# Fewer barriers between the spans of a two-layer decoder, and the next span's norm computed inside the down projection

## Chip, cores and metric

The kernel runs on one Trainium2 chip, on 8 cores at once. Each core works on two of the 16 batch entries and shares nothing with the others but the memory that they read from. The metric is the device time in microseconds (us) of the slowest core. Engines are named as in the profile: PE is TensorE's matmuls, PEld its weight loads, DVE VectorE, ACT ScalarE, POOL GpSimd, SP SyncE.

## What is computed

Two decoder layers over 2064 positions (16 meta tokens and 2048 inputs), width 1024. The reference, cut down:

```python
def hybrid_layer(h, ...):
    hn = rmsnorm(h, g_mix)
    z = hn @ w_in
    u, c_q, c_kv, k_rope, gate_a, gate_b = jnp.split(z, IN_OFFSETS, axis=-1)
    a = pool_mixer(u, pool_w, pool_scale)          # causal means over 2, 4, 8, 16 positions, then 128x128 products
    ...                                            # q, k, v from the normed latents, rope
    b = mla_attention(q_nope, q_rope, k_nope, k_rope, v)
    merged = jax.nn.sigmoid(gate_a) * (a @ w_pa) + jax.nn.sigmoid(gate_b) * (b @ w_pb)
    h = h + merged @ w_o
    hn = rmsnorm(h, g_ffn)
    h = h + (jax.nn.silu(hn @ w_gate) * (hn @ w_up)) @ w_down
    return h
# after both layers: rmsnorm(h, final_norm_g)[:, N_META:]
```

`rmsnorm` divides by the root of the mean square over the 1024 channels and multiplies by a gain.

## The kernel before

`hT` holds the state of one batch entry transposed, channels on the partitions (8 chunks of 128) and positions on the free axis, in float32, and stays on the chip. For each of the two entries and each of the two layers there are three phases:

1. Latents (lines 404 to 451): the norm and the latent projections, in blocks of 512 positions.
2. Attention (lines 455 to 547), head by head.
3. Pooling mixer, merge and feed-forward (lines 551 to 687), in three spans of 688 positions, each of two blocks of 344. A span does: the mixer norm (`norm_span(SM_GMIX)`, line 571); the pooling input projection (64 matmuls, lines 579 to 584), which ACT copies into `Ubf`; the pooling products (68 matmuls, lines 586 to 594); gates and merge (lines 607 to 629); the output projection (128 matmuls); the feed-forward norm (line 642); gate and up projections (704 matmuls); and the down projection (lines 670 to 677): for each of 8 output chunks `m` two groups of 22 matmuls of 344 columns, each group followed by one addition into `hT` on DVE. In layer 1 a final norm of both blocks follows (lines 678 to 686), and each normed block goes out from one buffer, `ost`, by a DMA on SP.

Every norm goes through `rms_block` (line 356), per block: ACT squares the 8 chunks into two small buffers in turn, PE sums each square with a matmul against ones, ACT takes Ln and Exp of the sum, DVE writes the 8 normed chunks (`scalar_tensor_tensor`, line 257).

Each engine runs its instructions in the order in which the program wrote them. The class `Prog` turns buffer objects (`Buf`, with their last writers and readers) into semaphore waits. `P.barrier()` makes PE, ACT, DVE and POOL wait for everything that all four have issued; it stands after phase 1 (line 452), after phase 2 (line 548) and after each span (line 687), there also on the output DMAs. Weights come as tiles through a ring of three buffers (`wtile`, line 283), each tile by a DMA issued by POOL when the buffer's last readers are done. PSUM has 8 banks, used in turn (`ps_next`).

The buffer objects of a span are made anew at its start, so they know nothing of the span before. `Ubf`, `aT` and `merged` lie on the same bytes as `actT`, the input of the down projection.

Of the kernel before, what the change touches and what calls it, by code (L numbers as in the profile page):

```python
# [15 lines left out]
KC = 8  # L16
# [19 lines left out]
BLK = 344  # L36
NSPAN = 3
SPAN = L // NSPAN
NBLK = SPAN // BLK

SM_GMIX, SM_GFFN, SM_PSC, SM_QG, SM_KVG, SM_GFIN, SM_N = 0, 8, 16, 20, 22, 23, 31
# [139 lines left out]
def build_program(stop_at=None):  # L181
# [12 lines left out]
    with ExitStack() as st:  # L194
        sbt = lambda n, s, d: st.enter_context(nc.sbuf_tensor("sb_" + n, s, d))
        hT_t = sbt("hT", [128, KC * L], F32)
        hT = hT_t[:, :].rearrange("p (c t) -> p c t", c=KC)
# [16 lines left out]
        P = Prog(nc)  # L214
# [21 lines left out]
        s_out = P.new_dma_sem()  # L236
# [3 lines left out]
        def MM1(out, lhsT, rhs, start, stop, reads=(), writes=(), inc=True):  # L240
            return P.op("pe", lambda e: e.matmul(out, lhsT, rhs, start=start, stop=stop), reads=reads, writes=writes, inc=inc)  # L241
# [7 lines left out]
        def ACT(out, in_, func, reads, writes, **kw):  # L249
            return P.op("act", lambda e: e.activation(out=out, in_=in_, func=func, **kw), reads=reads, writes=writes)  # L250

        def TT(out, in0, in1, op, reads, writes, extra=()):
            return P.op("dve", lambda e: e.tensor_tensor(out=out, in0=in0, in1=in1, op=op), reads=reads, writes=writes,  # L253
                        extra=extra)

        def STT(out, in0, scalar, in1, op0, op1, reads, writes):
            return P.op("dve", lambda e: e.scalar_tensor_tensor(out=out, in0=in0, scalar=scalar, in1=in1, op0=op0, op1=op1),  # L257
                        reads=reads, writes=writes)

        def TS(out, in0, scalar1, op0, reads, writes):  # L260
            return P.op("dve", lambda e: e.tensor_scalar(out=out, in0=in0, scalar1=scalar1, scalar2=None, op0=op0),
                        reads=reads, writes=writes)

        def RPOW(out, in_, pw, reads, writes, wbuf, scale=1.0, bias=0.0):
            ACT(out, in_, AF.Ln, reads=reads, writes=[wbuf], scale=scale, bias=bias)
            return ACT(out, out, AF.Exp, reads=[wbuf], writes=writes, scale=pw)
# [16 lines left out]
        def wtile(idx, used):  # L283
            i = wctr[0] % 3
            wctr[0] += 1
            DMA("pool", WB[i][:, :used], wst[idx, :, :used], wsem[i], writes=[WBB[i]])
            return WB[i], WBB[i]
# [3 lines left out]
        def ps_next():  # L291
            b = psring["banks"][psring["i"] % len(psring["banks"])]
            psring["i"] += 1
            return PS[b], PSB[b]

        def sm(l, col):
            return smalls[:, l * SM_N + col: l * SM_N + col + 1]
# [22 lines left out]
        srt = None  # L320
# [10 lines left out]
        hn = A3.alloc([KC * SPAN], BF16).rearrange("p (c t) -> p c t", c=KC)  # L331
# [3 lines left out]
        srt3 = None  # L335
        rstd3 = A3.alloc([BLK], F32)
        sq3 = [A3.alloc([BLK], BF16) for _ in range(2)]
# [3 lines left out]
        ost = A3.alloc([KC * BLK], F32).rearrange("p (c t) -> p c t", c=KC)  # L341
# [6 lines left out]
        merged = A3b.alloc([KC * SPAN], BF16).rearrange("p (c t) -> p c t", c=KC)  # L348
        aT = A3b.alloc([4 * SPAN], BF16).rearrange("p (c t) -> p c t", c=4)
# [6 lines left out]
        def rms_block(srcs, n, gcols, dsts, rd, wr, sq_bufs, sqB, srt_ap, rstd_ap, srtB, rstdB, inv_n=1.0 / D):  # L356
            nch = len(srcs)
            psA, psAB = ps_next()
            for c in range(nch):
                j = c % 2  # L360
                ACT(sq_bufs[j][:, :n], srcs[c], AF.Square, reads=rd, writes=[sqB[j]])
                MM1(psA[:, :n], ones[:, :], sq_bufs[j][:, :n], c == 0, c == nch - 1,
                    reads=[sqB[j], cb["ones"]], writes=[psAB], inc=True)
            RPOW(rstd_ap[:, :n], psA[:, :n], -0.5, reads=[psAB], writes=[rstdB], wbuf=rstdB, scale=inv_n, bias=EPS)
            for c in range(nch):
                STT(dsts[c], srcs[c], gcols[c], rstd_ap[:, :n], ALU.mult, ALU.mult,
                    reads=list(rd) + [rstdB, cb["smalls"]], writes=wr)

        def stop_check(s, l, ph):
            if stop_at == (s, l, ph):  # L370
                raise _Stop()

        def main_body():
          for s in range(NS):
# [9 lines left out]
            for l in range(DEPTH):  # L384
# [62 lines left out]
                for bi in range(len(T512)):  # L447
# [1 line left out]
                    if bi + 1 < len(T512):  # L449
                        p1_front(bi + 1)  # L450
                    p1_back(bi, zs)
                P.barrier()
                stop_check(s, l, 1)

                watt = [wtile(base + 1, 3072), wtile(base + 2, 3072)]
# [97 lines left out]
                for g in range(4):  # L553
                    TS(Wa[:, g, :], poolw[:, g, :], 1.0 / POOL_W[g], ALU.mult, reads=[cb["poolw"]], writes=[WaB])
                    TS(Wn[:, g, :], poolw[:, g, :], -1.0, ALU.mult, reads=[cb["poolw"]], writes=[WnB])
                for sp in range(NSPAN):
                    T0 = sp * SPAN
                    B3 = {k: Buf(k) for k in ["hn0", "hn1", "sq0", "sq1", "srt", "rstd", "U0", "U1", "A", "B", "y", "aT", "merged", "act",
                                              "sil0", "sil1", "sg0", "sg1", "sg2", "sg3", "mt0", "mt1", "mt2", "mt3", "ost", "t16", "hT"]}
                    blocks = [(b * BLK, BLK) for b in range(NBLK)]  # L560

                    def hnB(bo):
                        return B3["hn%d" % (bo // BLK)]

                    def norm_span(gcol):
                        for (bo, n) in blocks:
                            rms_block([hT[:, c, T0 + bo:T0 + bo + n] for c in range(KC)], n, [sm(l, gcol + c) for c in range(KC)],
                                      [hn[:, c, bo:bo + n] for c in range(KC)], [B3["hT"]], [hnB(bo)],
                                      sq3, [B3["sq0"], B3["sq1"]], srt3, rstd3, B3["srt"], B3["rstd"])

                    norm_span(SM_GMIX)
                    wp_t, wpB = wtile(base + 3, KC * 512)
                    wp = wp_t[:, :].rearrange("p (k c) -> p k c", k=KC)
                    UB = [B3["U0"], B3["U1"], B3["A"], B3["B"]]
                    if sp == 0:
# [10 lines left out]
                    for g in range(4):  # L586
                        wnd = POOL_W[g]
                        for (bo, n) in blocks:
# [4 lines left out]
                            TS(aT[:, g, bo:bo + n], ps[:, :n], sm(l, SM_PSC + g), ALU.mult,  # L593
                               reads=[psb, cb["smalls"]], writes=[B3["aT"]])
                        if sp == 0:
# [5 lines left out]
                            TT(tmp16[:, :], p1[:, :16], invc[:, g * 16:(g + 1) * 16], ALU.mult,  # L601
                               reads=[p1B, cb["invc"]], writes=[B3["t16"]])
                            TT(tmp16[:, :], tmp16[:, :], p2[:, :16], ALU.add, reads=[B3["t16"], p2B], writes=[B3["t16"]])
# [26 lines left out]
                    for half in range(2):  # L630
                        wo_t, woB = wtile(base + 12 + half, KC * 512)
                        wo = wo_t[:, :].rearrange("p (k c) -> p k c", k=KC)
                        for mm in range(4):
                            m = half * 4 + mm
# [4 lines left out]
                                TT(hT[:, m, T0 + bo:T0 + bo + n], ps[:, :n], hT[:, m, T0 + bo:T0 + bo + n], ALU.add,  # L639
                                   reads=[psb, B3["hT"]], writes=[B3["hT"]])  # L640
                    guard = P.now()
                    norm_span(SM_GFFN)
                    si = [0]

                    def ffn_job(wf, wfB, cc, c, bo, n):
# [24 lines left out]
                    for m in range(KC):  # L670
                        wd_t, wdB = wtile(base + 25 + m, FC * 128)
                        wd = wd_t[:, :FC * 128].rearrange("p (k c) -> p k c", k=FC)
                        for (bo, n) in blocks:
                            ps, psb = ps_next()
                            mm_group(ps[:, :n], [(wd[:, k, :], actT[:, k, bo:bo + n]) for k in range(FC)], [wdB, B3["act"]], psb)
                            TT(hT[:, m, T0 + bo:T0 + bo + n], ps[:, :n], hT[:, m, T0 + bo:T0 + bo + n], ALU.add,
                               reads=[psb, B3["hT"]], writes=[B3["hT"]])
                    if l == DEPTH - 1:
                        os_ = outT[s].rearrange("(c p) t -> p c t", p=128)
                        for (bo, n) in blocks:  # L680
                            t0 = T0 + bo
                            rms_block([hT[:, c, t0:t0 + n] for c in range(KC)], n, [sm(l, SM_GFIN + c) for c in range(KC)],
                                      [ost[:, c, :n] for c in range(KC)], [B3["hT"]], [ostB],
                                      sq3, [B3["sq0"], B3["sq1"]], srt3, rstd3, B3["srt"], B3["rstd"])
                            lo = max(t0, NM)
                            DMA("sp", os_[:, :, lo - NM:t0 + n - NM], ost[:, :, lo - t0:n], s_out, reads=[ostB])
                    P.barrier(extra=[("d", s_out, P.dma_sems[s_out])] if P.dma_sems[s_out] else [])
                stop_check(s, l, 3)
        try:
            main_body()  # L690
# [102 lines left out]
```

How the kernel before makes its waits and increments, by code:

```python
            def run(e, engine):  # L141
                for waits, fn, inc, dsi in self.ops[e]:
                    for (k, a, v) in waits:
                        engine.wait_ge(esem[a] if k == "e" else dsem[a], v)
                    if fn is None:
                        continue
                    ins = fn(engine)
                    if dsi is not None:
                        ins.then_inc(dsem[dsi], 16)
                    elif inc:
                        ins.then_inc(esem[e], 1)
```

## Time and profile before

| | us |
|---|---|
| median of two runs | 6549.44 |
| the two runs | 6215.61 and 6883.28 |
| the profiled execution's own time | 6215.9 |
| its span, slowest core (core 3) | 6214.4 |
| the eight cores' spans | 6190.6 to 6214.4 |
| PE busy | 5096.7 (82% of the span) |
| ACT busy | 2513.8 (40%) |
| DVE busy | 2134.1 (34%) |

A timeline row gives the start of a group of like instructions, its length, engine, line, operation, output and input, the count, and in brackets how long the engine had been idle before it and what released it. L241 is the matmul helper, L250 the ACT helper, L253 DVE's additions and products, L257 the norm's last step, L281 the DMA helper, so groups are told apart by their tiles: `ps<-sb_arena,sb_ones` is a norm's sum of squares, `sb_hT<-ps,sb_hT` the addition after a down projection group.

### The profile page before, as it was taken

Reading aid. Unit: us, or ns where it says so; the run is one execution under the profiler, and the core shown is the slowest. Engines: PE = TensorE matmul, PEld = TensorE weight load, DVE = VectorE, ACT = ScalarE, POOL = GpSimd, SP = SyncE. Lnnn points to the kernel's source line nnn. Section 1 sums busy time; section 2 is a strip of 40 time slices with the busy share of each in tenths; the row PEclk is TensorE's granted clock in tenths of the full one; section 3 lists DMA queues with packets and bytes.
Section 4 is the critical chain, followed back from the end, with each engine's and each line's share of the span. In section 5 each row is a group of like instructions: output and inputs, shape, how many; then the busy total and the mean of one; then the engine's idle time right before and its main releaser. Section 6 shows DMA issues by size and latency. Waiting matters only on the chain.

```text
span 6214.4 us, 101463 instructions; the slowest of 8 cores (6190.6 to 6214.4 us)
## 1 busy us (share of the span) xinstructions
PE 5096.7 (82%) x30452; PEld 2816.9 (45%) x30452; DVE 2134.1 (34%) x3957; ACT 2513.8 (40%) x5517; POOL 705.4 (11%) x1785
## 2 busy tenths in 40 slices
PE   3777898999577798989847778989986777989897
PEld 1333565655232365655513335656652333646465
DVE  3444323132444332323234443232324443323232
ACT  2778312121477721212127783121214776222121
POOL 0222100000122200000002220000001221000000
PEclk8899999999799898999969989999997999989898
DMA  3000454555000155545520004556540001555554
GB/s 80 1 1 1 82 98 90 95 95 91 11 1 1 20 95 99 92 94 95 94 82 1 1 1 89 92 89 108 91 81 11 1 1 26 98 95 97 100 92 90
DMA packets 81738, 385.85 MB, mean 62 GB/s; under 512 B 12864, under 2 KB 27328, under 8 KB 59072
## 3 DMA queue, kind: packets, MB, share of 16 engines
q0 software_dynamic: 55824, 344.55, 31.7%
q1 hardware_dynamic: 25392, 34.81, 1.7%
q8 instruction: 271, 4.44, 0.3%
q14 instruction: 251, 2.06, 0.1%
HBM read 707.08 MB, written 16.78 MB: 116 GB/s over the span
## 4 chain that ended last, share of the span: by engine, by line
PE 73%; ACT 10%; DVE 7%; issue 6%; DMA 2%; ACTq 1%; POOL 0%; DVEq 0%; POOLq 0%; SPq 0%
PE ps L241 73%; ACT sb_arena L250 10%; DVE sb_arena L257 5%; DMA outT<-sb_arena 1%; DVE sb_arena L275 1%; DMA sb_hT<-xT 1%; DVE sb_arena L253 1%; ACT L250 1%; ACTq L144 1%; DMA sb_wb<-wst 0%; POOL sb_arena L272 0%; DMA sb_hT<-metaT 0%; DVEq L144 0%; DVE sb_hT L253 0%; DVE ps L253 0%
## 5 line engine op out<-in xcount | busy, mean ns | idle before, releaser
L241 PE MATMUL ps<-sb_arena,sb_wb 128*128 128x344 bf16 (+2 forms) x20416 | 3279.9, 319 | 239.6 <-DVE sb_arena L257 106.0
L250 ACT ACTIVATE sb_arena<-ps 128x512 bf16<-128x512 f32 (+8 forms) x4388 | 1934.3, 503 | 2178.2 <-PE ps L241 1624.7
L241 PEld LDWEIGHTS ps<-sb_arena,sb_wb 128*128 128x128 bf16 x20416 | 2011.4, 99 | 1414.0 <-issue 418.2
L241 PE MATMUL ps<-sb_arena 128*128 128x512 bf16 (+5 forms) x6712 | 1449.5, 337 | 413.8 <-ACT sb_arena L250 260.7
L241 PEld LDWEIGHTS ps<-sb_arena 128*128 128x128 bf16 x6712 | 556.7, 100 | 1254.2 <-issue 1068.3
L253 DVE TENSOR_TENSOR sb_arena<-sb_arena,ps 128x344 bf16<-128x344 f32 (+2 forms) x928 | 470.0, 507 | 1394.3 <-PE ps L241 1069.5
L250 ACT ACTIVATE sb_arena<-sb_hT 128x344 bf16<-128x344 f32 (+2 forms) x640 | 288.6, 495 | 1256.2 <-DVE sb_hT L253 912.9
L272 POOL TENSOR_TENSOR sb_arena<-sb_arena,sb_tri 128x128 bf16<-128x128 bf16 (+2 forms) x1344 | 473.1, 370 | 1562.9 <-ACT sb_arena L250 1557.8
L241 PE MATMUL ps<-sb_arena,sb_ones 128*128 128x344 bf16 (+2 forms) x700 | 263.4, 411 | 436.9 <-ACT sb_arena L250 407.2
L275 DVE CAST sb_arena<-ps 64x512 bf16<-64x512 f32 (+3 forms) x832 | 468.5, 568 | 382.7 <-PE ps L241 368.3
L257 DVE SCALAR_TENSOR_TENSOR sb_arena<-sb_hT,sb_smalls,sb_arena 128x344 bf16<-128x344 f32 (+3 forms) x640 | 380.1, 594 | 605.5 <-ACT sb_arena L250 509.3
L281 POOL DMA_DIRECT2D sb_wb<-wst x372 | 197.0, 530 | 3363.0 <-PE ps L241 3072.1
L253 DVE TENSOR_TENSOR sb_bT<-ps,sb_arena 64x512 bf16<-64x512 f32 (+1 forms) x320 | 185.7, 580 | 801.2 <-ACT sb_arena L250 704.5
L253 DVE TENSOR_TENSOR sb_hT<-ps,sb_hT 128x344 f32<-128x344 f32 x384 | 198.2, 516 | 668.9 <-PE ps L241 668.9
L241 PEld LDWEIGHTS ps<-sb_arena,sb_ones 128*128 128x128 bf16 x700 | 69.9, 102 | 618.8 <-issue 614.4
L241 PE MATMUL ps<-sb_bT,sb_wb 128*128 128x344 bf16 x1536 | 255.3, 309 | 0.0
L250 ACT ACTIVATE sb_arena<-sb_arena 64x512 f32<-64x512 f32 (+4 forms) x440 | 236.0, 536 | 42.0 <-ACT sb_arena L250 2.0
L253 DVE TENSOR_TENSOR sb_arena<-ps,sb_rope 64x512 bf16<-64x512 f32 (+3 forms) x340 | 200.4, 590 | 34.5 <-DVE sb_arena L275 1.4
L241 PEld LDWEIGHTS ps<-sb_bT,sb_wb 128*128 128x128 bf16 x1536 | 150.3, 98 | 73.7
L250 ACT ACT_TABLE_LOAD x49 | 62.9, 1283 | 201.3 <-PE ps L241 165.1
L253 DVE TENSOR_TENSOR sb_arena<-sb_arena 128x344 bf16<-128x344 f32 x192 | 99.3, 517 | 20.7 <-DVE sb_arena L253 0.9
L269 POOL COPY sb_arena<-sb_arena 32x512 bf16<-32x512 bf16 (+1 forms) x60 | 31.4, 524 | 436.3 <-DVE sb_arena L253 432.5
(18 smaller groups left out, 259.6 us busy)
## 6 DMA issues: line engine op xcount, KB each, us to landing
sb_wb<-wst POOLq DMA_DIRECT2D x172, 1024.0 KB, 8.4
sb_wb<-wst POOLq DMA_DIRECT2D x96, 896.0 KB, 8.5
sb_wb<-wst POOLq DMA_DIRECT2D x96, 704.0 KB, 6.7
outT<-sb_arena SPq DMA_DIRECT2D x10, 1376.0 KB, 5.7
sb_hT<-xT SPq DMA_DIRECT2D x6, 2048.0 KB, 16.9
sb_wb<-wst POOLq DMA_DIRECT2D x8, 768.0 KB, 8.8
sb_hT<-xT SPq DMA_DIRECT2D x2, 1984.0 KB, 18.7
outT<-sb_arena SPq DMA_DIRECT2D x2, 1312.0 KB, 5.7
```

The costliest lines, as they stand in the source:

```text
L144: engine.wait_ge(esem[a] if k == "e" else dsem[a], v)
L241: return P.op("pe", lambda e: e.matmul(out, lhsT, rhs, start=start, stop=stop), reads=reads, writes=writes, inc=inc)
L250: return P.op("act", lambda e: e.activation(out=out, in_=in_, func=func, **kw), reads=reads, writes=writes)
L253: return P.op("dve", lambda e: e.tensor_tensor(out=out, in0=in0, in1=in1, op=op), reads=reads, writes=writes, extra=extra)
L257: return P.op("dve", lambda e: e.scalar_tensor_tensor(out=out, in0=in0, scalar=scalar, in1=in1, op0=op0, op1=op1), reads=reads, writes=writes)
L269: return P.op("pool", lambda e: e.tensor_copy(out=out, in_=in_), reads=reads, writes=writes)
L272: return P.op("pool", lambda e: e.tensor_tensor(out=out, in0=in0, in1=in1, op=op), reads=reads, writes=writes)
L275: return P.op("dve", lambda e: e.tensor_copy(out=out, in_=in_), reads=reads, writes=writes)
L281: return P.dma(eng, lambda e: e.dma_start(out=out, in_=in_), sem, reads=reads, writes=writes, extra=extra)
```

## The change

The barrier after phase 1 is emitted only in a debugging mode that is off here. The barrier after a span stays after the third span alone; the other two record the instruction counts at that point (`span_guard`), and in the next span ACT and DVE, but not PE and POOL, wait for those counts before the first write to `Ubf`. The norm's small buffers, `hn` and `hT` get buffer objects that live through the three spans. The mixer norm of the next span is issued inside the down projection, after its chunk `m == 4`.

```diff
-                P.barrier()
+                if stop_at is not None:
+                    P.barrier()
                 stop_check(s, l, 1)
...
+                BN = {k: Buf(k) for k in ["hn0", "hn1", "sq0", "sq1", "srt", "rstd"]}
+                hTB3 = [Buf("hTs%d" % i) for i in range(NSPAN)]
...
+                def norm_span(gcol, spi):
+                    for (bo, n) in blocks:
+                        rms_block([hT[:, c, spi * SPAN + bo:spi * SPAN + bo + n] for c in range(KC)], n,
+                                  [sm(l, gcol + c) for c in range(KC)],
+                                  [hn[:, c, bo:bo + n] for c in range(KC)], [hTB3[spi]], [hnB(bo)],
+                                  sq3, [BN["sq0"], BN["sq1"]], srt3, rstd3, BN["srt"], BN["rstd"])
...
-                    norm_span(SM_GMIX)
+                    B3["hT"] = hTB3[sp]
+
+                    if sp not in pre_normed:
+                        norm_span(SM_GMIX, sp)
+                    if span_guard:
+                        P.wait_all("act", span_guard[0])
+                        P.wait_all("dve", span_guard[0])
+                        span_guard.clear()
                     wp_t, wpB = wtile(base + 3, KC * 512)
...
                             TT(hT[:, m, T0 + bo:T0 + bo + n], ps[:, :n], hT[:, m, T0 + bo:T0 + bo + n], ALU.add,
                                reads=[psb, B3["hT"]], writes=[B3["hT"]])
+                        if m == 4 and sp + 1 < NSPAN:
+                            norm_span(SM_GMIX, sp + 1)
+                            pre_normed.add(sp + 1)
...
-                    P.barrier(extra=[("d", s_out, P.dma_sems[s_out])] if P.dma_sems[s_out] else [])
+                    if sp + 1 < NSPAN:
+                        span_guard.append(P.now())
+                    else:
+                        P.barrier(extra=[("d", s_out, P.dma_sems[s_out])] if P.dma_sems[s_out] else [])
```

How the order of instructions moves. First PE in layer 0, from the output projection of a span (128 matmuls) to the pooling products of the next; `sb_ones` rows are a norm's sums of squares, and 1056 is the 704 of gate and up with the 352 of down:

```order
 L241 MATMUL ps<-sb_arena,sb_wb 128x344 x128
 L241 MATMUL ps<-sb_arena,sb_ones 128x344 x16
-L241 MATMUL ps<-sb_arena,sb_wb 128x344 x1056
+L241 MATMUL ps<-sb_arena,sb_wb 128x344 x924
 L241 MATMUL ps<-sb_arena,sb_ones 128x344 x16
-L241 MATMUL ps<-sb_arena,sb_wb 128x344 x64
+L241 MATMUL ps<-sb_arena,sb_wb 128x344 x196
 L241 MATMUL ps<-sb_arena 128x344 x68
```

The 16 sums now stand 132 down projection matmuls (chunks 5 to 7) earlier; those 132 and the next span's 64 follow without a break in the order.

Then the same stretch of PE in layer 1, where a final norm stands between the spans:

```order
-L241 MATMUL ps<-sb_arena,sb_wb 128x344 x1056
-L241 MATMUL ps<-sb_arena,sb_ones 128x344 x32
+L241 MATMUL ps<-sb_arena,sb_wb 128x344 x924
+L241 MATMUL ps<-sb_arena,sb_ones 128x344 x16
+L241 MATMUL ps<-sb_arena,sb_wb 128x344 x132
+L241 MATMUL ps<-sb_arena,sb_ones 128x344 x16
 L241 MATMUL ps<-sb_arena,sb_wb 128x344 x64
 L241 MATMUL ps<-sb_arena 128x344 x68
```

Of 32 sums between the down projection and the pooling input projection, 16 stay (the final norm's) and 16 moved ahead of chunk 5.

Last ACT in layer 1, at the end of the same stretch, with what its instructions wait for (`s_dve` is DVE's count, `s_act` ACT's own): the rows from `sb_hT` are the mixer norm's squares of the second block, the first removed row from `ps` is its Ln, and the rows from `ps` behind it are the eight copies into `Ubf`:

```order
-L250 ACTIVATE sb_arena<-sb_hT 128x344 x2
-L250 ACTIVATE sb_arena<-sb_hT 128x344 [waits s_act,s_pe] x6
-L250 ACTIVATE sb_arena<-ps 128x344 [waits s_pe,s_dve]
-L250 ACTIVATE sb_arena<-sb_arena 128x344 [waits s_act]
-L250 ACTIVATE sb_arena<-ps 128x344 [waits s_pe,s_dve]
+L250 ACTIVATE sb_arena<-ps 128x344 [waits s_act,s_dve,s_pe]
 L250 ACTIVATE sb_arena<-ps 128x344 [waits s_pe] x3
 L250 ACTIVATE sb_arena<-ps 128x344 [waits s_pe,s_act] x4
```

The norm is gone from here (it stands behind the last Silu now), and the first copy waits for the guard's counts, which in layer 1 take in DVE's last step of the final norm.

## Rows read from the trace of the kernel before

**Rows 1.** Spans of the cores, with TensorE's mean granted clock.
```profile
core 3: 6214.4 us, clock 0.907
die 0 (median of its cores): 6201.5 us, clock 0.908
die 1 (median of its cores): 6200.6 us, clock 0.906
```
**Rows 2.** The page's chain that ended last, by engine.
```profile
PE 73%; ACT 10%; DVE 7%; issue 6%; DMA 2%; ACTq 1%; POOL 0%; DVEq 0%; POOLq 0%; SPq 0%
```
**Rows 3.** Timeline of PE and ACT, first entry, layer 0, between spans 1 and 2.
```profile
947.78 0.69 PE L241 MATMUL ps<-sb_arena,sb_ones 128*128 128x344 bf16 x2 [1.42 <-ACT sb_arena L250]
...
951.82 1.28 ACT L250 ACT_TABLE_LOAD   x1 [0.67 <-PE ps L241]
...
954.68 0.82 PE L241 MATMUL ps<-sb_arena,sb_ones 128*128 128x344 bf16 x2 [2.94 <-ACT sb_arena L250]
...
958.20 0.83 PE L241 MATMUL ps<-sb_arena,sb_ones 128*128 128x344 bf16 x2 [0.34 <-ACT sb_arena L250]
...
959.73 11.59 PE L241 MATMUL ps<-sb_arena,sb_wb 128*128 128x344 bf16 x64 [0.71 <-DVE sb_arena L257]
...
966.35 2.08 ACT L250 ACTIVATE sb_arena<-ps 128x344 bf16<-128x344 f32 x5 [5.63 <-DVE sb_arena L275]
```
**Rows 4.** Windows from last down matmul to pooling products; layer 0, then layer 1; busy by engine.
```profile
946.36:971.16 24.80, 17.45 (x81) 8.63 (x82) 9.82 (x18) 12.94 (x28) 1.59 (x3) 0.72 0.60 117
1237.39:1262.11 24.72, 17.27 (x81) 8.40 (x81) 9.82 (x18) 12.84 (x28) 1.59 (x3) 0.72 0.59 117
2442.36:2496.51 54.15, 24.64 (x97) 10.45 (x97) 19.04 (x34) 21.78 (x48) 1.59 (x3) 0.59 0.44 105
2763.04:2817.43 54.39, 24.37 (x97) 10.44 (x97) 19.04 (x34) 21.62 (x48) 1.59 (x3) 0.59 0.45 105
```
**Rows 5.** The same windows view within rows 3; before the DMA columns stands the granted clock.
```profile
949.00:950.00 1.00, 0.57 (x3) 0.19 (x2) 0.00 (x0) 0.83 (x3) 0.24 (x1) 1.00 0.78 66
...
951.00:953.00 2.00, 0.74 (x2) 0.11 (x1) 0.00 (x0) 1.33 (x2) 0.00 (x0) 0.50 1.10 225
...
963.00:964.00 1.00, 1.00 (x6) 0.45 (x4) 0.90 (x2) 0.00 (x0) 0.00 (x0) 0.50 0.96 203
...
965.00:966.00 1.00, 1.00 (x9) 0.68 (x7) 0.90 (x2) 0.00 (x0) 0.00 (x0) 1.00 0.04 7
```
**Rows 6.** Timeline, layer 1, between spans 1 and 2 of the first entry.
```profile
2443.89 0.57 PE L241 MATMUL ps<-sb_arena,sb_ones 128*128 128x344 bf16 x2 [1.53 <-ACT sb_arena L250]
...
2454.60 0.83 PE L241 MATMUL ps<-sb_arena,sb_ones 128*128 128x344 bf16 x2 [0.35 <-ACT sb_arena L250]
...
2456.31 11.76 SPq L281 DMA_DIRECT2D outT<-sb_arena  x2
...
2462.27 5.34 DVE L257 SCALAR_TENSOR_TENSOR sb_arena<-sb_hT,sb_smalls,sb_arena 128x344 f32<-128x344 f32 x8 [6.04 <-DMA outT<-sb_arena]
2473.00 0.87 ACT L250 ACTIVATE sb_arena<-sb_hT 128x344 bf16<-128x344 f32 x2 [15.63 <-DMA outT<-sb_arena]
...
2484.71 11.97 PE L241 MATMUL ps<-sb_arena,sb_wb 128*128 128x344 bf16 x64 [0.44 <-DVE sb_arena L257]
```
**Rows 7.** PE's timeline, layer 0: feed-forward after its norm, then the down projection.
```profile
1080.72 104.17 PE L241 MATMUL ps<-sb_arena,sb_wb 128*128 128x344 bf16 x704 [0.61 <-DVE sb_arena L257]
1185.90 51.49 PE L241 MATMUL ps<-sb_arena,sb_wb 128*128 128x344 bf16 x352 [1.01 <-DVE sb_arena L253]
```
**Rows 8.** Timeline at the barrier after phase 1: POOL's last copies and its DMAs, then PE.
```profile
142.80 0.76 POOL L269 COPY sb_arena<-sb_arena 32x16 bf16<-32x16 bf16 x3 [0.47 <-DVE sb_arena L253]
144.10 1.05 POOL L281 DMA_DIRECT2D sb_wb<-wst  x2 [0.54 <-POOL sb_arena L269]
...
151.62 1.44 PE L241 MATMUL ps<-sb_arena,sb_wb 128*128 128x512 bf16 x3 [11.06 <-DMA sb_wb<-wst]
```
**Rows 9.** The page's DMA issues: KB each, median us to landing.
```profile
sb_wb<-wst POOLq DMA_DIRECT2D x96, 896.0 KB, 8.5
```

More of the change, by code:

```diff
@@ L555, in main_body, with hnB @@
                     TS(Wn[:, g, :], poolw[:, g, :], -1.0, ALU.mult, reads=[cb["poolw"]], writes=[WnB])
+                BN = {k: Buf(k) for k in ["hn0", "hn1", "sq0", "sq1", "srt", "rstd"]}
+                hTB3 = [Buf("hTs%d" % i) for i in range(NSPAN)]
+                blocks = [(b * BLK, BLK) for b in range(NBLK)]
+                pre_normed = set()
+                span_guard = []
+                def hnB(bo):
+                    return BN["hn%d" % (bo // BLK)]
+                def norm_span(gcol, spi):
[4 more added lines that the diff above has]
+                                  sq3, [BN["sq0"], BN["sq1"]], srt3, rstd3, BN["srt"], BN["rstd"])
@@ L556, in main_body @@
                 for sp in range(NSPAN):
                     T0 = sp * SPAN
[L558 to L569, printed above, removed]
-                    norm_span(SM_GMIX)
+                    B3 = {k: Buf(k) for k in ["U0", "U1", "A", "B", "y", "aT", "merged", "act",
+                                              "sil0", "sil1", "sg0", "sg1", "sg2", "sg3", "mt0", "mt1", "mt2", "mt3", "ost", "t16"]}
@@ L641, in main_body @@
                     guard = P.now()
-                    norm_span(SM_GFFN)
+                    norm_span(SM_GFFN, sp)
                     si = [0]
@@ L683, in main_body @@
                                       [ost[:, c, :n] for c in range(KC)], [B3["hT"]], [ostB],
-                                      sq3, [B3["sq0"], B3["sq1"]], srt3, rstd3, B3["srt"], B3["rstd"])
+                                      sq3, [BN["sq0"], BN["sq1"]], srt3, rstd3, BN["srt"], BN["rstd"])
                             lo = max(t0, NM)
                             DMA("sp", os_[:, :, lo - NM:t0 + n - NM], ost[:, :, lo - t0:n], s_out, reads=[ostB])
-                    P.barrier(extra=[("d", s_out, P.dma_sems[s_out])] if P.dma_sems[s_out] else [])
+                    if sp + 1 < NSPAN:
+                        span_guard.append(P.now())
+                    else:
+                        P.barrier(extra=[("d", s_out, P.dma_sems[s_out])] if P.dma_sems[s_out] else [])
                 stop_check(s, l, 3)
```

## The prediction, made before the changed kernel ran

> **What bounds the kernel now.** I read the cores first: all eight lie within 24 us and the two dies are level in span and clock [rows 1], so the kernel is undisturbed in this execution and one core stands for all. The profiled execution took 6215.9 us (span 6214.4), which agrees with the lower of the two timed runs, 6215.61; the median, 6549.44, is the mean of that and 6883.28. The sum below is made against 6215.9. The chain of waits is PE for 73% [rows 2], so what can be saved is time in which PE waits for others. The change touches phase 3 at the eight places between spans (two entries, two layers, two places each) and the barrier after phase 1 at four, so next come the timelines there.
>
> Inside a span PE is dense: the down projection runs 352 matmuls in 51.49 us [rows 7], 146.3 ns each. At the pause between spans of layer 0 [rows 3] PE ends its last down matmul at 946.36, does the 16 sums of the mixer norm at the pace of ACT's squares, and starts the pooling input projection at 959.73. From the last down matmul to the pooling products it is 24.8 and 24.7 us, in layer 1 54.2 and 54.4 us [rows 4]. In layer 1 [rows 6] the final norm comes first, its second block waits for the output DMA of the first (one buffer), then the barrier waits for the second DMA (DVE ends at 2467.61, ACT resumes at 2473.00), and only then the mixer norm begins.
>
> **The moved norm still stops PE.** PE takes instructions in order, and the 16 sums are now between chunks 4 and 5 of the down projection. ACT has nothing to do in a down projection, so the first two squares of the first block are ready. The other six wait for PE's sums (two square buffers), then come Ln with a table load of 1.28 us, Exp, and the second block's squares. That is the stretch from the first sum at 947.78 to the last at 959.03: 3.95 us, a gap of 2.94, and 4.35, so 11.2 us [rows 3]. What falls away is 1.4 us ahead of it (addition and first square) and 0.7 us behind it (PE waited for DVE's eight steps, which now run under chunk 5). Those 16 steps delay DVE's additions there by up to 6 us; PE doesn't feel it, since eight PSUM banks are six groups of 3.2 us deep.
>
> **The clock.** In the pause of layer 0 the granted clock was 1.00 (2.4 GHz) up to 950, fell to 0.50 (1.2 GHz) after 4 us of sparse sums, and was back at 1.00 about 4.3 us after dense matmuls began [rows 5]. The 64 matmuls there took 11.59 us [rows 3] where 64 at 146.3 ns [rows 7] are 9.36, so a re-entry costs 2.2 us. The moved norm is as sparse and as long, so chunk 5 pays this: the moved norm costs PE 11.2 + 2.2 = 13.4 us.
>
> **Layer 0.** After the last down matmul PE goes straight on: its normed input is there and the weight tile is in (POOL issues it when chunk 5 has been read, 12.8 us earlier, and a tile lands in 8.5 us [rows 9]). The guard holds ACT's first copy until the last addition, some 0.7 us, and the copies (0.4 us each [rows 3]) are faster than the groups of 1.17 us. So 9.4 us remain of the 24.8, plus 13.4: 22.8. Gain 2.0 us, four times: 8 us.
>
> **Layer 1.** With the last down matmul at 0, the final norm's first sum comes at 1.5 as before [rows 6]. Its table load has gone with the moved norm, so all after it is 1.28 earlier: last sum over at 11.8 (2455.43 - 2442.36 - 1.28), first block out at 12.7, its DMA landed and DVE started on the second block at 2462.27 - 2442.36 - 1.28 = 18.6, and ended 5.34 later, 24.0. PE starts the 64 pooling input matmuls at 11.8 and needs no copy until all are done, since eight groups fill eight banks: over by 23.4 even at the slow clock (11.6). But the guard counts DVE's last step, so the halo copy and ACT's first copy wait until 24.0, and the first pooling product needs the fifth copy: 24.3 + 2.1 (five copies [rows 3]) + 0.2 = 26.6. The output DMA of the second block and the whole second norm are gone from this path. 26.6 + 13.4 = 40.0 against 54.3 [rows 4]. Gain 14.3 us, four times: 57 us.
>
> **After phase 1.** POOL issues the attention weights behind its own last copies in either version; it was 0.54 us behind them [rows 8], and PE waited for the landing. At most that half us goes: 2 us in four places. The barrier hid nothing else.
>
> **Sum:** 8 + 57 + 2 = 67; 6215.9 - 67 = **6149 us**, 1.1% less. DMA traffic and instruction counts are the same. The unknown terms: PE's idle time before the pooling products in layer 1 is 3 us, and with it the clock may fall again, 0 to 2.2 us in four places; in rows 5 the clock held for 4 us of sparse work, so I take 0. Re-entry in chunk 5: between 0, if the clock doesn't fall, and 4.3 (twice the value, as long again at 1.2 GHz); I take 2.2, from the stretch most like it. Together -18 to +26, so 6131 to 6175, and some 0.3% of scatter.
>
> **A rule that speaks against the change.** Core 3 is granted 1.00 in dense stretches [rows 5], and the mean clocks of both dies are 0.91 with the pauses in them [rows 1]. The Trainium skill (TensorE: Matmul & The Clock Gate, section Part 1: The HAM clock gate) says of a peak-current limiter that three cores of a die in dense matmuls bring the die to 13/16 of its clock, 1.95 GHz. By it the 352 down matmuls would take 62 us, as an estimate from that page, and removing pauses would only give the limiter more to hold; the trace, with 51.49 us for them, disagrees in this execution.
>
> **Rivals.**
> *Nothing gained in layer 1* (8%). If PE can't run the 64 matmuls under the final norm, because a bank or the weight tile is late, the 57 us fall by 9.4 to 11.6 in each of four places, to about 15: 6190. Against it: the last tiles are issued at chunk ends, not at the barrier, and the banks were emptied in the down projection.
> *The clock stays low after the moved norm* (4%), the case on the other side. If after the stop in chunk 4 the granted clock stayed at 0.50 until the final norm or the next phase, 132 matmuls would take 292 ns, 19.3 us more each time instead of 2.2: 8 x 17.1 = 137 us, so 6286, slower than before. It decides from 8.4 us of extra loss at a place on (67/8), that is 21 us at 1.2 GHz. Against it: after the feed-forward norm, an equal stop, 704 matmuls took 104.17 us [rows 7], 1.2 us over 146.3 ns each.
> *A whole die is held to a lower clock* (4%), since the pauses are fewer. The price from the two timed runs is their ratio, 6883.28 / 6215.61 = 1.107: 6149 x 1.107 = 6810. For it: a run of the same program was that long. Against it: PE's pauses shrink by only 1% of the time.
> *The sums in the down projection cost nearly nothing* (2%), if PE stopped only for a few us: up to 8 x 13.4 = 107 us more, 6042. Against it: order on PE and two square buffers.
>
> **Numbers.** The forecast has 82%: 6149. The range is 6110 to 6200: it takes in the forecast with its unknown terms and scatter and the first rival, and leaves the other three out, with some of the forecast's own tails. About 2% (124 us) is what a measurement tells from no change: faster by more needs nearly twice the sum, 4%; within 2% 91%; slower 5%.
>
> **What would show it.** In the new trace PE should have a stop of 11 us with 16 `sb_ones` sums 19 us ahead of the last down matmul, with the clock at 0.50 into chunk 5; in layer 0 no idle time from the down projection through the pooling products; in layer 1 one pause of 13 us, 64 matmuls, then 3 us until ACT's fifth copy, released by DVE's last final-norm step. POOL's tiles must be issued during chunks 5 to 7. It is wrong if PE waits for a weight tile or a bank there, if ACT's copies are released by a DMA, or if the stretch in layer 1 is not near 27 us.

## The result and the profile after

| | before | changed |
|---|---|---|
| profiled execution, us | 6215.9 | 6151.36 |
| span of its slowest core, us | 6214.4 | 6149.8 |
| median of all runs, us | 6629.02 (10 runs) | 6317.42 (11 runs) |
| lowest and highest, us | 6215.61, 6883.28 | 6147.67, 6805.87 |
| changed / before, undisturbed runs | | 0.9895 (95%: 0.9871 to 0.9919) |

In 8 of these 10 runs of the kernel before and in 7 of the 11 of the changed one, a die held at a lower granted clock made the time longer, so the medians of all runs are not compared, and the ratio is that of the others. Those are 6148 to 6155 us for the changed kernel: 1.05% faster, where 1.1% was forecast. That is less than 2%, but the whole interval lies below 1.

The cores and the chain of waits of the changed kernel answer to [rows 1] and [rows 2]:

```profile
core 3: 6149.8 us, clock 0.913
die 0 (median of its cores): 6139.2 us, clock 0.914
die 1 (median of its cores): 6137.8 us, clock 0.914
```
```profile
PE 74%; ACT 11%; issue 6%; DVE 6%; DMA 2%; ACTq 1%; POOL 0%; DVEq 0%; POOLq 0%; SPq 0%
```

PE's timeline of the changed kernel between spans 1 and 2 of layer 0 answers to [rows 3]. The `sb_ones` rows are the moved norm's sums:

```profile
924.99 0.46 PE L241 MATMUL ps<-sb_arena,sb_ones 128*128 128x344 bf16 x2
926.02 0.69 PE L241 MATMUL ps<-sb_arena,sb_ones 128*128 128x344 bf16 x2 [0.58 <-ACT sb_arena L250]
...
931.96 0.73 PE L241 MATMUL ps<-sb_arena,sb_ones 128*128 128x344 bf16 x2 [3.04 <-ACT sb_arena L250]
...
935.48 0.82 PE L241 MATMUL ps<-sb_arena,sb_ones 128*128 128x344 bf16 x2 [0.35 <-ACT sb_arena L250]
936.10 29.83 PE L241 MATMUL ps<-sb_arena,sb_wb 128*128 128x344 bf16 x196
965.77 10.11 PE L241 MATMUL ps<-sb_arena 128*128 128x344 bf16 x68
```

The stop is inside the down projection and takes 11.1 us (924.99 to 936.10). After it nothing interrupts PE: 132 down and 64 pooling input matmuls run as one row, and the pooling products follow. The clock, in the windows view of this stop (the column before the last two is the granted clock), answers to [rows 5]:

```profile
927.00:929.00 2.00, 1.43 (x4) 0.40 (x4) 0.00 (x0) 1.16 (x3) 0.00 (x0) 0.77 0.71 110
929.00:931.00 2.00, 0.00 (x0) 0.00 (x0) 0.00 (x0) 1.90 (x3) 0.00 (x0) 0.50 1.00 203
...
936.10:938.00 1.90, 1.90 (x8) 1.03 (x8) 0.57 (x1) 0.95 (x2) 0.00 (x0) 0.50 0.04 9
938.00:939.00 1.00, 1.00 (x8) 0.60 (x6) 0.89 (x2) 0.00 (x0) 0.00 (x0) 0.85 0.00 0
939.00:940.00 1.00, 1.00 (x9) 0.66 (x8) 0.83 (x2) 0.00 (x0) 0.00 (x0) 1.00 0.00 0
```

It fell to 1.2 GHz in the stop and was back 2.2 us into chunk 5. In the next place of layer 0 it took longer, since the same 196 matmuls took 31.07 us; PE's timeline there, from the start of the down projection to the pooling products:

```profile
1180.65 32.24 PE L241 MATMUL ps<-sb_arena,sb_wb 128*128 128x344 bf16 x220 [1.09 <-DVE sb_arena L253]
...
1223.71 31.07 PE L241 MATMUL ps<-sb_arena,sb_wb 128*128 128x344 bf16 x196
1254.62 10.11 PE L241 MATMUL ps<-sb_arena 128*128 128x344 bf16 x68
```

In layer 1 (timeline of PE, SP, DVE and ACT, same two spans) the rows answer to [rows 6]:

```profile
2446.38 0.69 PE L241 MATMUL ps<-sb_arena,sb_ones 128*128 128x344 bf16 x2 [1.42 <-ACT sb_arena L250]
...
2455.36 0.82 PE L241 MATMUL ps<-sb_arena,sb_ones 128*128 128x344 bf16 x2 [0.35 <-ACT sb_arena L250]
2456.02 11.75 PE L241 MATMUL ps<-sb_arena,sb_wb 128*128 128x344 bf16 x64
2456.83 11.67 SPq L281 DMA_DIRECT2D outT<-sb_arena  x2
...
2462.70 5.34 DVE L257 SCALAR_TENSOR_TENSOR sb_arena<-sb_hT,sb_smalls,sb_arena 128x344 f32<-128x344 f32 x8 [5.95 <-DMA outT<-sb_arena]
...
2468.42 2.91 ACT L250 ACTIVATE sb_arena<-ps 128x344 bf16<-128x344 f32 x8 [10.26 <-DVE sb_arena L275]
2470.42 11.77 PE L241 MATMUL ps<-sb_arena 128*128 128x344 bf16 x68 [2.65 <-ACT sb_arena L250]
```

The 64 input matmuls now run while DVE waits for the first output DMA, and PE's pause moved behind them: 2.65 us until ACT's copies, which wait for DVE's last final-norm step by way of the halo copy. From the last down matmul (2444.96) to the pooling products it is 25.5 us.

### The profile page after: what moved, and what is told of

It is laid out like the page before. It is cut to its first block, busy times and chain, and to the rows that moved or that the text cites. A ratio compares the mean times of both kernels' runs of the same rounds, so it can differ in the third digit from the quotient of the medians.

```text
span 6149.8 us, 101447 instructions; the slowest of 8 cores (6132.2 to 6149.8 us)
## 1 busy us (share of the span) xinstructions
PE 5102.9 (83%) x30452; PEld 2822.9 (46%) x30452; DVE 2134.4 (35%) x3957; ACT 2512.6 (41%) x5517; POOL 705.2 (11%) x1785
## 4 chain that ended last, share of the span: by engine, by line
PE 74%; ACT 11%; issue 6%; DVE 6%; DMA 2%; ACTq 1%; POOL 0%; DVEq 0%; POOLq 0%; SPq 0%
PE ps L241 74%; ACT sb_arena L250 10%; DVE sb_arena L257 4%; DVE sb_arena L275 1%; DMA sb_hT<-xT 1%; DMA outT<-sb_arena 1%; DVE sb_arena L253 1%; ACT L250 1%; ACTq L144 1%; DMA sb_wb<-wst 0%; POOL sb_arena L272 0%; DMA sb_hT<-metaT 0%; DVEq L144 0%; DVE sb_hT L253 0%; DVE ps L253 0%
## 5 line engine op out<-in xcount | busy, mean ns | idle before, releaser
L253 DVE TENSOR_TENSOR sb_arena<-sb_arena 128x344 bf16<-128x344 f32 x192 | 99.3, 517 | 20.4 <-DVE sb_arena L253 0.5
```

## The experiments

All were run beside the kernel before, each group on one chip: e1 to e4 on one, the repeat and e5 to e7 on another, e8 alone on a third. The times are of the same kind of run as the 6148 to 6155 us above, and values apart from the others are given singly. The kernel before took 6211 to 6224 us in the first group, 6215 to 6221 and once 6286 in the second, 6217 and 6236 in the third, so differences between groups, such as e1 to e4 against the changed kernel, are uncertain by some us.

| kernel | expected | measured, us | ratio to before (95%) |
|---|---|---|---|
| e1 guard only | 6166 | 6167 to 6169 | 0.9920 (0.9902 to 0.9938) |
| e2 early norm only | 6290 | 6290 to 6291 | 1.0117 (1.0096 to 1.0139) |
| e3 sums spread | 6062 | 6067 to 6069 | 0.9761 (0.9743 to 0.9778) |
| e4 two output buffers | 6125 | 6120 to 6122 | 0.9845 (0.9824 to 0.9866) |
| changed kernel again | 6147 to 6155 | 6148 to 6152, 6184, 6222 | 0.9908 (0.9843 to 0.9974) |
| e5 stop filled | 6135 | 6133 to 6136 | 0.9841 (0.9757 to 0.9925) |
| e6 = e3 + e4 | 6036 | 6037 to 6039 | 0.9686 (0.9619 to 0.9752) |
| e7 all norms spread | 5906 | 6018, 6021, 6074 | 0.9701 (0.9566 to 0.9835) |
| e8 = e7, buffers by block | 5970 | 5972 (twice), 5994 | 0.9609 (0.9509 to 0.9709) |

**e1, the guard without the early norm.**

```diff
-                        if m == 4 and sp + 1 < NSPAN:
-                            norm_span(SM_GMIX, sp + 1)
-                            pre_normed.add(sp + 1)
```

> The changed kernel without the early norm: the mixer norm stands at the span's start again, the barriers stay replaced by the guard. Theory (PE waits for itself behind the norm's sums, and the barrier's cost in layer 1 is the wait for the second output DMA): layer 0 stays at about 24.8 us from last down matmul to pooling products, layer 1 falls from 54.3 to 41 to 43 us, since Ln of the mixer norm still waits for DVE's last final-norm step but not for the DMA; 6166 us, so about three quarters of the gain are the guard's. Rival (the early norm is what pays, the barriers cost nothing): about 6216.

6167 to 6169 us: of the 65 us gained, some 49 are the guard's. Most of it is in layer 1: from the start of the down projection to the pooling products it took 94.2 us (2384.49 to 2478.67) against 105.6 before, in layer 0 75.0 against 76.3. In its timeline the second final-norm block still waits for the first DMA, but the mixer norm no longer waits for the second:

```profile
2455.37 5.34 DVE L257 SCALAR_TENSOR_TENSOR sb_arena<-sb_hT,sb_smalls,sb_arena 128x344 f32<-128x344 f32 x8 [5.71 <-DMA outT<-sb_arena]
2460.80 0.46 ACT L250 ACTIVATE sb_arena<-ps 128x344 f32<-128x344 f32 x1 [5.62 <-DVE sb_arena L257]
...
2467.43 11.41 PE L241 MATMUL ps<-sb_arena,sb_wb 128*128 128x344 bf16 x64 [0.61 <-DVE sb_arena L257]
```

The mixer norm's Ln (2460.80) starts right behind DVE's last final-norm step. The wait for the second DMA was 5.4 us before (2467.61 to 2473.00 [rows 6]); the rest of the 11.5 us comes from the first block's squares and sums, which now run ahead of DVE's last steps. The rival that the early norm is what pays has fallen.

**e2, the early norm without the guard.**

```diff
-                    if sp + 1 < NSPAN:
-                        span_guard.append(P.now())
-                    else:
-                        P.barrier(extra=[("d", s_out, P.dma_sems[s_out])] if P.dma_sems[s_out] else [])
+                    P.barrier(extra=[("d", s_out, P.dma_sems[s_out])] if P.dma_sems[s_out] else [])
```

> The changed kernel with the full barrier back at every span's end, the early norm kept. Theory: the early norm costs PE its 13.4 us in any case, and with the barrier the first weight tile is issued only after it, 8.5 us before it lands, which the norm at the span's start used to hide; so layer 0 goes to about 35 us (stop included) from 24.8, layer 1 to 63 from 54.3, and the time to about 6290 us, slower than before the change. Rival (the early norm is what pays): 6151 to 6170.

6290 us, 73 us or 1.2% slower than before. The cover that the norm at the span's start gave to the first weight tile is gone; layer 0, core 4, on the undisturbed die:

```profile
951.98 1.59 POOL L281 DMA_DIRECT2D sb_wb<-wst  x3 [31.79 <-DVE sb_arena L275]
960.04 11.04 PE L241 MATMUL ps<-sb_arena,sb_wb 128*128 128x344 bf16 x64 [9.35 <-DMA sb_wb<-wst]
970.92 10.11 PE L241 MATMUL ps<-sb_arena 128*128 128x344 bf16 x68
```

So the early norm needs the guard: alone it loses 73 us, on top of the guard it gains 17.

**e3, the sums spread over the down projection.** The call after chunk 4 is gone. Behind each of the first eight groups stands a call for two squares and sums; behind every fourth group it also does Ln, Exp and the eight DVE steps of a block:

```diff
+                            if m < 4 and sp + 1 < NSPAN:
+                                norm_step(2 * m + bo // BLK, sp + 1, st_)
+                                pre_normed.add(sp + 1)
```

> The changed kernel with the 16 squares and sums of the early norm spread over the first eight groups of the down projection, two behind each group, instead of all behind chunk 4. Theory (the stop of 11.2 us and the clock's 2.2 are on PE's path and only 16 x 0.146 = 2.3 us are work): PE never waits in the down projection, 8 x 11.1 = 89 us less than the changed kernel, 6062 us. Rival (the stop's price is small, or comes back later as another wait): 6130 to 6151.

6067 to 6069 us, 83 less than the changed kernel, so the price of the moved norm was on PE's path, 10.4 us a place. PE in layer 0:

```profile
893.78 3.37 PE L241 MATMUL ps<-sb_arena,sb_wb 128*128 128x344 bf16 x22 [1.09 <-DVE sb_arena L253]
896.99 0.46 PE L241 MATMUL ps<-sb_arena,sb_ones 128*128 128x344 bf16 x2
...
921.61 0.46 PE L241 MATMUL ps<-sb_arena,sb_ones 128*128 128x344 bf16 x2
921.90 35.16 PE L241 MATMUL ps<-sb_arena,sb_wb 128*128 128x344 bf16 x240
956.90 10.11 PE L241 MATMUL ps<-sb_arena 128*128 128x344 bf16 x68
```

No `sb_ones` row has idle time ahead of it, and 240 matmuls run at 146 ns.

**e4, a second output buffer.** The second block is written to `ostb`, on the bytes of the merge's scratch tiles, and goes out on a semaphore of its own (the main line of the edit):

```diff
...
+                            o_, oB, oS = (ost, ostB, s_out) if bo == 0 else (ostb, ost2B, s_out2)
...
```

> The changed kernel with a second output buffer for the final norm's second block (on the bytes of the merge's scratch tiles), so that it doesn't wait for the first block's DMA. Theory (that DMA sets the guard in layer 1): the pooling products follow the 64 input matmuls without a pause and at the full clock, 4.2 us less in four places, and the end of each entry comes 4.4 us earlier, together 26: 6125 us. Rival (ACT's copies or PE bound it anyway): 6151.

6120 to 6122 us, 30 less than the changed kernel. DVE's second block doesn't wait for the DMA, and PE has no pause before the pooling products (layer 1, core 1):

```profile
2447.69 11.78 PE L242 MATMUL ps<-sb_arena,sb_wb 128*128 128x344 bf16 x64
...
2449.98 5.34 DVE L258 SCALAR_TENSOR_TENSOR sb_arena<-sb_hT,sb_smalls,sb_arena 128x344 f32<-128x344 f32 x8 [1.52 <-ACT sb_arena L251]
...
2459.31 10.11 PE L242 MATMUL ps<-sb_arena 128*128 128x344 bf16 x68
```

**The changed kernel again.**

> The changed kernel once more, unaltered, beside the next three on one chip. Theory: 6147 to 6155 us where no die is held to a lower clock. Rival for the long executions (fewer pauses make a die more likely to be held): markedly more of this kernel's executions are long than of the kernel before's, where 8 of 10 were.

6148 to 6152 us, twice somewhat more (6184 and 6222). On this chip 7 of its 12 runs were over 1.5% above the fastest, and 11 of the 17 of the kernel before; with the first result that is 14 of 23 against 19 of 27. The rival that fewer pauses make long executions more frequent has nothing for it, though such counts can't rule out a small difference.

**e5, the stop filled with matmuls.** Nothing uses their products.

```diff
+                        if bo:
+                            fill(18)
...
+                            if c < KC - 1:
+                                fill(2)
```

> The changed kernel with idle time inside the early norm filled: two extra matmuls on constants behind each sum and 18 between the blocks, into a spare bank, results unused (344 columns each, 0.146 us at 2.4 GHz). Theory (2.2 us of each stop's price are the clock's fall to 1.2 GHz and its return in chunk 5): the granted clock stays 1.00, chunk 5 runs at 146 ns a matmul, 8 x 2 = 16 us less than the changed kernel, 6135 us; the stop itself stays 11 us. Rival (the clock has no part, or the filling delays the sums by as much): 6151 or more.

6133 to 6136 us, 16 less than the changed kernel, although PE does more. The windows view of its stop (926.97 to 937.65) has 1.00 throughout, and what follows is dense from the start, 196 matmuls in 28.74 us where the changed kernel took 29.83 and 31.07:

```profile
930.00:932.00 2.00, 2.00 (x15) 1.26 (x15) 0.00 (x0) 1.47 (x2) 0.00 (x0) 1.00 0.92 163
932.00:934.00 2.00, 1.58 (x11) 0.88 (x10) 0.58 (x1) 1.89 (x5) 0.00 (x0) 1.00 0.68 138
...
936.00:938.00 2.00, 2.00 (x13) 0.96 (x14) 1.73 (x3) 1.17 (x3) 0.00 (x0) 1.00 0.00 0
```

**e6, e3 and e4 together.**

> The spread norm and the second output buffer together. Theory (they act at different places): the two differences add up, -84 and -31 as measured singly, so 6036 us. Rival (one covers part of the other): 6045 to 6067.

6037 to 6039 us: -83 and -30 add up to the measured -113. Neither gain covers part of the other.

**e7, all norms of phase 3 spread.** Feed-forward and final norm sum each chunk behind the groups of the next:

```diff
+                                if m > 0:
+                                    acc_sum(m - 1, bo // BLK, sp)
...
-                    norm_span(SM_GFFN, sp)
+                    for b_ in range(2):
+                        acc_sum(KC - 1, b_, sp)
+                        acc_pow(b_)
...
```

> As before, and the feed-forward and final norms as well are summed while their input is made: each chunk's square and sum follow the next chunk's groups in two banks kept for them, a second buffer for the root, the halo copy on POOL, the guard taken ahead of the final norm. Theory (what is left of a norm's stop is last addition, one square, Ln with table load, Exp and eight DVE steps, 8.2 us of 13.7 for the feed-forward norm in 12 places; in layer 1 PE goes on after 1.5 us instead of 11.2 in 4 places, and ends come 8 us earlier in 2): 66 + 48 + 16 us less than the spread kernel with two buffers, 5906 us. Rival (ACT and DVE get in each other's way with six banks instead of eight): 5960 to 6036.

6018 to 6021 us, only 18 less than e6 where 130 were expected. My working had left out that the sums, once hidden in the stop, now lengthen the output projection, and they also waited. PE on core 2, undisturbed:

```profile
1042.81 0.31 PE L242 MATMUL ps<-sb_arena,sb_ones 128*128 128x344 bf16 x1 [0.22 <-ACT sb_arena L251]
...
1061.46 0.31 PE L242 MATMUL ps<-sb_arena,sb_ones 128*128 128x344 bf16 x1 [1.39 <-ACT sb_arena L251]
1064.70 0.44 PE L242 MATMUL ps<-sb_arena,sb_ones 128*128 128x344 bf16 x1 [2.94 <-ACT sb_arena L251]
1069.87 104.92 PE L242 MATMUL ps<-sb_arena,sb_wb 128*128 128x344 bf16 x704 [4.72 <-DVE sb_arena L258]
```

From the start of the output projection (1035.90) to the feed-forward it is 34.0 us; in the kernel before it was 32.6 (1048.16 to 1080.72). That turns the expected 66 us into a loss of 17, and the final norm's sums lengthen the down projection of layer 1 by 2.3 us in six places, 14 more; of the 112 us missing, some 15 are left. Behind the pooling products of layer 1 PE now waits 1.6 to 2.8 us for ACT, 8.6 in four places, and in the two of these places looked at in e6 it has no such wait; some 6 us stay unexplained.

**e8, e7 with buffer objects by block.**

```diff
-                hTB3 = [[Buf("hT%d_%d" % (i, c)) for c in range(KC)] for i in range(NSPAN)]
+                hTB3 = [[[Buf("hT%d_%d_%d" % (i, c, b)) for b in range(2)] for c in range(KC)] for i in range(NSPAN)]
```

> As e7, but the buffer objects of the state are kept per chunk and block, where e7's per chunk made each block's square wait for the other block's addition too. Theory (in e7 the output projection took 24.2 us instead of 18.8: 2.3 for the 16 sums and some 3 of waits for squares, and the norm's stop then fell only from 13.7 to 9.8): the output projection takes 21.3 us and the stop 8.7, 4 us less in 12 places, so 5970 us. Rival (the waits were for something else, the six banks or DVE): 6015 to 6020 as e7.

5972 us, 3.9% faster than before (2.9 to 4.9%) and the fastest version, 48 less than e7. The instructions on PE are those of e7; only the waits differ. The sums inside the output projection no longer wait:

```profile
1052.49 0.62 PE L242 MATMUL ps<-sb_arena,sb_ones 128*128 128x344 bf16 x2
1056.04 0.45 PE L242 MATMUL ps<-sb_arena,sb_ones 128*128 128x344 bf16 x1 [2.94 <-ACT sb_arena L251]
1061.21 8.99 PE L242 MATMUL ps<-sb_arena,sb_wb 128*128 128x344 bf16 x45 [4.72 <-DVE sb_arena L258]
```

The same stretch (1031.93 to 1061.21) is 29.3 us, 3.3 less than in the kernel before. What is left is Ln with its table load, Exp, and DVE's eight steps.

## Why the prediction held in its sum and failed in its range

- **The sum.** Forecast 67 us, and the two profiled executions differ by 64.5. From the start of a down projection to the pooling products it took in the second place of layer 0 76.2 us before (from 1185.90 [rows 7] to 1262.11 [rows 4]) and 74.0 after (1180.65 to 1254.62): 2.2 gained, 2.0 forecast. All four places of layer 0 gained 3.4, 2.2, 2.4 and 3.8, together 11.8 against 8. In layer 1 the gap behind the last down matmul fell from 54.2 to 25.5 (26.6 forecast); its four places gained 16.8, 16.1, 13.6 and 15.0, and the slower pooling products took back 1.7, 1.7, 2.7 and 0, so 55.5 are left against 57. That makes 67.3; what lengthened the rest of the program by 3 us was not looked for.
- **The moved norm still stops PE**: 11.1 us measured, 11.2 forecast; with its clock term 13.4. e3 takes away 10.4 a place and keeps 2.3 of work (16 x 0.146): 12.7 together. Shown.
- **The clock.** 2.2 us a re-entry forecast. Behind the eight stops the matmuls took 0.9 to 2.3 us longer than the same rows of e5, 1.5 on average. e5, whose stop is also 0.3 us shorter (10.7), got back 16 us, 2.0 a place. Shown, and somewhat smaller than forecast. The term that I set to 0 and left open up to 2.2, the clock falling again before the pooling products in layer 1, came in three of the four places: 68 products took 11.77, 11.77 and 12.84 us instead of 10.11, together 6 us. So that term was mis-sized.
- **The guard in layer 1** waits for the last final-norm step and so for the first output DMA: e4 took that away and gained 30 us, 26 expected. PE's pause ahead of the 64 matmuls was 11.1 us (2444.96 to 2456.02), as the sum had it (11.8), where the last paragraph of the prediction names 13.
- **After phase 1**: 0.54 us behind POOL's copies [rows 8] became 0.26 here; at most 0.3 us a place, and no run tested it by itself.
- **The rivals on PE.** The first (nothing gained in layer 1) failed, since no tile or bank was late. The second (the clock stays low) failed, since the 132 matmuls took 20.4 to 21.6 us and not 38.6. The last (the sums cost nearly nothing) failed by e3.
- **The step that failed** is the base that I chose, with the chance of 4% for the case that a whole die is held to a lower clock. The sum starts from 6215.9, the level of the lower of two timed runs (6215.61), when the other, one in two, was 10.7% longer, and the range had no room for it. The runs show that such an execution is no rare case: 7 of 11 of the changed kernel here, so the median of all runs, 6317.42, lies outside 6110 to 6200 for that reason alone. My step tied the case to this change (fewer pauses); the runs show it in both kernels about as often, 19 of 27 before and 14 of 23 after. That the median came as near as 6317.42 is chance: the kernel before had medians from 6316 to 6629 in its four groups, so a range for the median had to reach to some 6600, whatever the change. The sum speaks of undisturbed runs alone.
- **The page's rule.** The Trainium skill (TensorE: Matmul & The Clock Gate, section Part 1: The HAM clock gate) has three dense cores bring a die to 13/16 of its clock. I set that aside on the strength of one undisturbed execution, and that was rash. In the undisturbed profiles of both kernels the dense stretches are at 1.00 and no core is ever at 0.81, against the rule. But three profiles, of e2, e4 and e7, have a longer die, and its cores are at 0.81 in dense stretches, in agreement with it. e2, windows view of core 0, then of core 2, both on the longer die, each in us from its own start:

```profile
1200.00:1220.00 20.00, 20.00 (x115) 12.36 (x114) 3.83 (x8) 3.20 (x7) 0.61 (x2) 0.81 0.51 96
6260.00:6280.00 20.00, 20.00 (x139) 13.43 (x138) 4.49 (x9) 3.84 (x9) 1.16 (x3) 1.00 0.79 143
...
1200.00:1220.00 20.00, 20.00 (x139) 13.41 (x138) 3.10 (x6) 0.00 (x0) 1.59 (x3) 1.00 0.77 116
6260.00:6280.00 20.00, 20.00 (x115) 12.36 (x114) 3.59 (x7) 3.44 (x8) 0.53 (x1) 0.81 0.57 106
```

In 20 us 139 matmuls run at 1.00 and 115 at 0.81; core 0's 704 feed-forward matmuls took 123.23 us where those of core 4, on the other die, took 104.10. The cores change in pairs. In e2 cores 0 and 1 have 0.81 in their dense stretches for their first 1.6 ms, cores 2 and 3 for their last 1.6; in e4 it is the first 3.5 of one pair and the last 3.5 of the other, in e7 the first 3.9 and the last 3.7. That would fit two pairs of a die that start apart and are held while both run, and a die would then stay at 1.00 where they hardly meet. It is argued and not shown, since no view gives one core's start against another's; what decides between short and long executions stays open.

## What to carry to other kernels

A norm moved under dense work is not hidden if its small matmuls stand together in PE's order: it costs the same wait there, and spreading its steps between the groups brings it down to the matmuls themselves, 2.3 us a place here. Before a barrier goes, list what each side of it waited for; here the guard in its place was worth 49 of 65 us, and the same norm moved with the barrier kept cost 73, since at its old place it had covered the next weight tile. Dependencies kept per tile actually read can be worth as much as the order of the instructions (e8 against e7, 48 us). And when one of two timed runs is 10% longer than the other, forecast which of the two is meant, or both.

## What the runs showed of the hardware

Filling a stop with matmuls whose results are dropped made the kernel 16 us faster: the granted clock stayed at 1.00 (2.4 GHz) in place of 0.50. And in the changed kernel a pause of 2.65 us in PE, behind 11.75 us of dense work, was followed by 1.7 us of loss in the pooling products, though the clock was at 1.00 before it (windows of layer 1, clock in the column before the last two):

```profile
2467.00:2468.00 1.00, 0.77 (x6) 0.29 (x3) 0.90 (x2) 0.00 (x0) 0.00 (x0) 1.00 0.00 0
2468.00:2470.40 2.40, 0.00 (x0) 0.01 (x1) 0.23 (x2) 1.98 (x6) 0.53 (x1) 1.00 0.57 199
2470.40:2472.00 1.60, 1.58 (x8) 0.91 (x9) 0.57 (x2) 0.93 (x3) 0.00 (x0) 0.65 1.04 312
2472.00:2473.00 1.00, 1.00 (x5) 0.57 (x4) 0.69 (x2) 0.00 (x0) 0.00 (x0) 0.50 1.37 214
```

The clock held through the pause and fell when PE was dense again. The length of the pause alone does not decide this. In the last place of layer 1 a pause of 3.37 us lost nothing:

```profile
5841.40:5844.70 3.30, 0.00 (x0) 0.02 (x1) 1.01 (x3) 1.99 (x6) 0.53 (x1) 1.00 0.50 56
5844.70:5847.00 2.30, 2.29 (x16) 1.57 (x17) 1.17 (x3) 0.92 (x3) 0.00 (x0) 1.00 1.06 181
```

In e5 a pause of 0.42 us left it at 1.00.

The granted clock of the long executions is a third value beside 0.50 and 1.00: 0.81 in dense stretches, on the cores of one die.
